# Sixteen modulation tiles of the first layer's head moved from TensorE matmuls to VectorE multiply-adds

## The reference, cut to what matters

```python
shift, scale, gate = jnp.split(jax.nn.silu(cond) @ w_mod + b_mod, 3, axis=-1)
h = rmsnorm(x, norm_g) * (1 + scale) + shift
q, k, v, z_a, xbc, z_s, dt_f, dt_b, g_a, g_s = split_cols(h @ w_in, IN_SPLITS)
```

## Time and profile before

| what | value |
|---|---|
| median of 3 runs | 2772.99 us (2772.13 to 2773.8) |
| the profiled execution | 2771.82 us, of which span 2769.8 us |
| PE busy | 2716.9 us (98% of the span) |
| DVE busy | 1965.2 us (71%) |
| ACT busy | 1481.7 us (53%) |
| HBM read and written | 226 GB/s over the span |
| granted TensorE clock, mean | 0.997 of full speed |

### The profile page before, as it was taken

How to read it: one execution, slowest core, us unless ns; L and a number is a source line. 1 busy time by engine, 2 the same in 40 slices (tenths; PEclk the granted TensorE clock), 3 DMA queues, 4 the chain that set the end, 5 groups by cost and what they waited for, 6 DMA issues and landing times.

```text
span 2769.8 us, 39481 instructions
## 1 busy us (share of the span) xinstructions
PE 2716.9 (98%) x15824; PEld 2325.3 (84%) x15824; DVE 1965.2 (71%) x2292; ACT 1481.7 (53%) x2145; POOL 172.1 (6%) x242
## 2 busy tenths in 40 slices
PE   7999999999999999999999999999999999999998
PEld 4898898888887888877779998889888888988886
DVE  2487888887997455599975788888866644555555
ACT  3366877785333455534335577687744344545443
POOL 0000101101000000000010011110110000000000
PEclk9999999999999999999999999999999999999999
DMA  9956666566887645578985566566566654555665
GB/s 394 344 179 213 226 223 206 207 221 240 316 305 258 200 141 166 191 287 293 336 303 172 203 220 221 198 225 223 191 222 242 243 199 158 174 161 178 203 220 167
DMA packets 175670, 627.89 MB, mean 227 GB/s; under 512 B 21028, under 2 KB 23332, under 8 KB 175104
## 3 DMA queue, kind: packets, MB, share of 16 engines
q1 hardware_dynamic: 154944, 557.19, 57.4%
q0 software_dynamic: 10672, 33.30, 4.1%
q10 hardware_dynamic: 9872, 34.89, 4.0%
HBM read 611.37 MB, written 13.93 MB: 226 GB/s over the span
## 4 chain that ended last, share of the span: by engine, by line
PE 84%; DVE 9%; issue 2%; DMA 2%; ACT 1%; SPq 0%; DVEq 0%; POOLq 0%; POOL 0%; ACTq 0%
PE PM L472 17%; PE PM L484 17%; PE PM L473 17%; PE PM L488 7%; PE PM L477 7%; PE PM L478 7%; PE A L764 6%; DVE arena L549 3%; DVE Zt L549 2%; DVE w_l L450 2%; DMA Zt<-in_w_mod 2%; PE PM L761 1%; DVE X L1568 1%; PE A L761 1%; ACT w_h L445 1%
## 5 line engine op out<-in xcount | busy, mean ns | idle before, releaser
L450 DVE TENSOR_TENSOR w_l<-raw,w_h 128x1024 fp32r<-128x1024 f32 (+1 forms) x880 | 1059.0, 1220 | 680.2 <-ACT w_h L445 673.3
L445 ACT ACTIVATE w_h<-raw 128x1024 fp32r<-128x1024 f32 (+1 forms) x880 | 904.9, 1046 | 802.1 <-PE PM L484 546.3
L472 PE MATMUL PM<-w_h,hT_h 128*128 128x512 f32 x1408 | 563.5, 400 | 2.1 <-issue 1.9
L473 PE MATMUL PM<-w_h,hT_l 128*128 128x512 f32 x1408 | 549.3, 390 | 0.0
L477 PE MATMUL PM<-hT_h,w_h 128*128 128x256 f32 x1920 | 479.1, 287 | 3.3 <-DVE X L1568 1.7
L478 PE MATMUL PM<-hT_l,w_h 128*128 128x256 f32 x1920 | 470.3, 283 | 0.0
L472 PE MATMUL PM<-w_h,Z 128*128 128x512 f32 x1016 | 399.3, 393 | 1.1 <-issue 0.8
L473 PE MATMUL PM<-w_h,Z 128*128 128x512 f32 x1016 | 395.7, 389 | 0.0
L484 PE MATMUL PM<-w_l,hT_h 128*128 128x512 f32 x1408 | 377.8, 390 | 3.0 <-DVE w_l L450 3.0
L477 PEld LDWEIGHTS PM<-hT_h,w_h 128*128 128x128 f32 x1920 | 367.2, 191 | 11.3 <-issue 6.9
L478 PEld LDWEIGHTS PM<-hT_l,w_h 128*128 128x128 f32 x1920 | 367.8, 192 | 2.1 <-issue 1.4
(11 more groups left out here) (204 smaller groups left out, 2230.5 us busy)
## 6 DMA issues: line engine op xcount, KB each, us to landing
raw<-in_w_in SPq DMA_DIRECT2D x608, 512.0 KB, 4.4
raw<-in_w_ps SPq DMA_DIRECT2D x128, 512.0 KB, 4.5
Zt<-in_w_mod SPq DMA_DIRECT2D x96, 512.0 KB, 13.2
arena<-in_w_mod SPq DMA_DIRECT2D x80, 512.0 KB, 6.4
Zt<-acs_scratch ACTq DMA_DIRECT2D x64, 512.0 KB, 4.8
raw<-in_w_pa SPq DMA_DIRECT2D x64, 512.0 KB, 4.1
raw<-in_w_out SPq DMA_DIRECT2D x64, 512.0 KB, 5.7
arena<-in_states POOLq DMA_DIRECT2D x16, 512.0 KB, 7.2
```

Source lines behind the costliest of these rows:

```text
L445: act.activation(w_h[:, k % RING, :, 0:n], half_raw(k, n), ACT.Copy).then_inc(hi_ready, 1)
L450: dve.tensor_tensor(w_l[:, k % RING, :, 0:n], half_raw(k, n), w_h[:, k % RING, :, 0:n].bitcast(F32), ALU.subtract).then_inc(lo_ready, 1)
L472: pe.matmul(tok_out(s), hi[:, kt, tk], wh, start=kt == 0, stop=False, skip_group_check=True)
L473: pe.matmul(tok_out(s), lo[:, kt, tk], wh, start=False, stop=False, skip_group_check=True)
```

## The change

In blocks 2 and 3 the tiles with odd kt (33, 35, ..., 47 and 49, 51, ..., 63: sixteen tiles) go through `tile_add` on DVE, into accumulators in the two halves of `X`. The even tiles stay with PE, and accumulate in `A` as before. Behind half 11 and half 19 PE runs `mod_sum` for the block, which adds DVE's accumulators onto what the even tiles left in the bank (`start` is false for it). ACT's copy of the block waits for that sum. On DVE the adds stand behind the low part of the same half as they stood behind on PE. SP's loads keep their order.

```diff
 def on_dve(m):
-    q = m // KT
-    return q == 11 or 3 < q < 10
+    q, kt = divmod(m, KT)
+    return q == 11 or 3 < q < 10 or q in (2, 3) and kt % 2 == 1
...
+SUMMED = (2, 3, 4, 5, 6, 7, 8, 9, 11)
...
         def mod_sums(q, s):
+            if q in (2, 3):
+                return X[:, 2 * MOD_N * (3 - q) + s * MOD_N:2 * MOD_N * (3 - q) + (s + 1) * MOD_N]
...
             held = tile_loaded(dve, m)
+            if first and q in (2, 3):
+                dve.wait_ge(s_("xT_copied"), 4)
...
                     mm = pe.matmul(A[32 * j:32 * j + 32, 3, 0:256], ones2[:, s, :], mod_sums(q, s)[:, j * 256:(j + 1) * 256],
-                                   start=s == 0, stop=s == 1, skip_group_check=True)
+                                   start=s == 0 and q > 3, stop=s == 1, skip_group_check=True)
...
-            if q < 4 or q == 10:
+            if q not in SUMMED:
                 act.wait_ge(mod_used, max(i for i, m in enumerate(PE_TILES) if m // KT == q) + 1)
             else:
-                act.wait_ge(s_("mod_summed"), q - 3 - (q == 11))
+                act.wait_ge(s_("mod_summed"), SUMMED.index(q) + 1)
...
                 if KT <= m < GROUP_TILES:
-                    sp.wait_ge(mod_used, m - Z_SLOTS + 1)
+                    tile_done(sp, m - Z_SLOTS)
...
                     if L == 0:
                         for m in Z_RUN.get(at, ()):
-                            mod_tile(pe, m)
+                            if not on_dve(m):
+                                mod_tile(pe, m)
+                        if at in (11, 19):
+                            mod_sum(pe, 2 + at // 16)
...
                     lo_half(dve, base + lc, 2 * g + ii, N if lc else 2 * NH)
+                    if L == 0:
+                        for m in Z_RUN.get(at, ()):
+                            if on_dve(m):
+                                tile_add(dve, m)
                     for step in st.get(at, ()):
                         step()
```

More of the change, by code:

```diff
@@ L141, in on_dve @@
 def on_dve(m):
-    q = m // KT
-    return q == 11 or 3 < q < 10
-DVE_TILES = [m for m in RAW_TILES.values() if on_dve(m)]
-PE_TILES = list(range(GROUP_TILES)) + [m for m in RAW_TILES.values() if not on_dve(m)]
+    q, kt = divmod(m, KT)
+    return q == 11 or 3 < q < 10 or q in (2, 3) and kt % 2 == 1
+DVE_TILES = [m for m in range(GROUP_TILES) if on_dve(m)] + [m for m in RAW_TILES.values() if on_dve(m)]
+SUMMED = (2, 3, 4, 5, 6, 7, 8, 9, 11)
+PE_TILES = [m for m in range(GROUP_TILES) if not on_dve(m)] + [m for m in RAW_TILES.values() if not on_dve(m)]
 PE_TILES = sorted(PE_TILES + list(range(FILLERS, FILLERS + KT)))
@@ L537, in tile_add @@
             held = tile_loaded(dve, m)
+            if first and q in (2, 3):
+                dve.wait_ge(s_("xT_copied"), 4)
             if first and q == 6:
-                dve.wait_ge(s_("mod_summed"), 1)
+                dve.wait_ge(s_("mod_summed"), SUMMED.index(4) + 1)
             if first and q == 9:
```

## The result

The changed kernel takes 2784.11 us (median of five runs, 2782.38 to 2785.0); the kernel before, on the same chip beside it, 2772.13 us (five runs, 2771.45 to 2773.8). The ratio is 1.0043 [1.0031, 1.0055], so 12.0 us slower. The forecast was 2778.2 us with a range to 2781.8: right in sign, but +5.2 us are less than half of the 12.0. The profiled execution took 2782.38 us, the fastest of the five, with a span of 2780.5 us: +10.7 us against the span of before.

What follows compares the result with a forecast made beforehand. The prediction took tile 63's landing as bounding the head, with DVE becoming the bound after the change: half 20 starts at 122.5 instead of 117.4, +5.1, plus 0.1 handover, +5.2 us, 2778.2 against the median; range 2775.2 to 2781.8.

Steps and rivals of the forecast that it cites:

- The work taken off PE: Head, blocks 2 and 3: net 6.4 us less PE work, worth 0 by itself because tile 63 lands no sooner.
- The price of an add: On DVE: 2.39 us per added tile, 1.32 for a block's first, assumed the same from `Zt` as from `arena`.
- DVE's cover: PE's idling of 5.7 us from 63.2, before tile 32, costs 0, since DVE does not need that PE work.
- The deep hollow: Load queue at half 17: late issue at 91.9 leaves it empty, so all that follows lands 1.7 us later.
- the queue stands still from 92.3 to 94.0: Half 17's load goes out at 91.9 as the queue runs empty; 2.1 us until data flows, later landings 1.7 us late.
- The term of 1.7 + 0.5 us: Load queue delay: 1.7 us at half 17 and a further 0.5 us at half 20, whose load waits for half 15.
- my chain: DVE's sequence of adds, low parts and waits from tile 33 at 63.3 to the last add's end at 121.4.
- the rule of five slots: Half 17's load may go out only when the low part of half 12 is done, moving it from 79.1 to 91.9.
- The lower one: Lower bound: no queue gap, DVE waits only for tile 63, then adds and sum; +2.9 us, perhaps +2 after later waits.
- The upper one: Upper bound: the queue gap at half 17 is 2 us longer, giving +7.2 us, or +9 with the clock.
- gap or clock worse: Rival: half 17's queue gap 1 to 2 us longer, or clock falls before the last sum; +6.8 to +9, chance 0.27.
- 0 for the last sum: PE's clock after about 2.8 us of idling before the last sum: 0 or +1.6 us, taken as 0.

Runs made afterwards that it cites:

- the last runs: Changed kernel with tiles 13 and 15 of both blocks kept on PE: 2778.92 us; with tile loads one half earlier 2773.47 us, two halves earlier 2772.99 us.
- tiles_early2: Changed kernel with the tile loads of blocks 2 and 3 two halves earlier in SP's order: 2775.49 us, 1.0012.
- late_raw: Kernel before, with SP waiting one half longer for a slot for the loads of halves 10 to 23: 2773.36 us, 1.0004.
- only_block3: Changed kernel with only block 3's eight odd tiles on DVE, block 2's staying on PE: 2780.15 us, 1.0031.
- defer2: Changed kernel with every odd tile added two halves later on DVE: 2781.98 us, 1.0035.

## Why the prediction was half right

| step | forecast | measured |
|---|---|---|
| DVE stands at tile 33 until | 63.3 | 63.15 |
| `mod_scale` of block 1 | 68.9 | 68.46 |
| end of the adds of block 2 | 90.8 | 93.5 |
| load of half 17 goes out | 91.9 | 94.77 |
| tile 51 has landed | 96.8 | 100.66 |
| end of the adds of block 3 | 121.4 | 127.3 |
| half 20 starts on PE | 122.5 | 128.5 |
| `mod_cols` of block 3 | 125.6 | 131.45 |

**Right.** The work taken off PE was worth nothing, by the last runs too. DVE became the engine that bounds the head, from its stop at tile 33 on. The price of an add, 2.40 us against 2.39, holds for reads from `Zt`. The late start of block 2's tiles on PE lay under DVE's cover: DVE waits for neither ACT nor PE between 59 and 128 us. The deep hollow came where it was forecast, at half 17, and cost 2.1 us against 1.7. Behind 131 us all is a constant shift.

**The step that failed** is "the queue stands still from 92.3 to 94.0", with all before it taken as full and 0.5 us for all behind it. The term of 1.7 + 0.5 us measured 8.1, by the landing of tile 63: 3.4 us before half 17 where I had 0, 2.1 at half 17, and 2.6 behind it where I had 0.5. Up to `mod_scale` of block 1 my chain was right, and it implied the number that shows the error: the low part of half 7 done near 72.3 (66.2 + 2.39 + 2.53 + 1.14), measured 72.1. Half 12's load waits for it, and had gone out at 64.36 before. I applied the rule of five slots at half 17 and not at halves 12 and 13. Half 13's waits for the low part of half 8 and went out at 76.10 instead of 65.91. So fewer loads came in from 70 to 84 us, DVE stood 2.6 us for tiles 43 and 45, and the load of half 17 went out 2.9 us later than I had it. The miss of 5.9 us at the end of the adds comes apart as: 2.9 us at half 17's issue; 1.0 us because tile 51 landed 5.9 us behind that issue and not 4.9; 1.7 us of waits for tiles 59 and 61 (1.49 and 0.22), that is the same loop at halves 20 to 22, which went out at 106.84 and later, where I had 0.5 us and no wait; 0.3 us of small differences over 26 us.

**The bounds.** The lower one, +2.9 us with a queue that never runs empty, is near what tiles_early2 measured (+3.2), but by luck: I had two adds and the sum behind tile 63's landing at 116.86, and there tile 63 lands at 113.78 and DVE's own work ends the head. The upper one, +7.2 and +9 with the clock, took one gap and made it 2 us longer. A gap that stops the engine which must close it isn't bounded by one gap's length. Here it came back: hollows from 70, 94 and 106 us on. The rival "gap or clock worse" had the right mechanism and was priced at one turn.

**The clock.** I took 0 for the last sum, and 0 it was in the profiled execution, which is luck, since I had one row on each side and no reason to choose. PE idled 3.19 us before 127.47 and the windows behind it stayed at 1.00, as this one of the changed kernel shows, set beside one under DVE's cover:

```profile
127.50:129.00 1.50, 1.50 (x20) 0.92 (x21) 1.50 (x2) 0.39 (x2) 0.00 (x0) 1.00 0.04 11
68.00:74.00 6.00, 5.20 (x27) 4.42 (x28) 5.93 (x15) 1.67 (x3) 0.00 (x0) 0.50 0.76 285
```

But the equal idle of 3.18 us before 93.66 was followed by 0.76 and then 0.50 at 94 to 98 us (windows above): the clock was 1.00 from 94 to 95 us and 0.54 from 95.0 to 95.5, so it fell when PE had been at work again for more than 1 us. And in the kernel before, 2.8 us had been enough at 38.75. The Trainium skill's "No PE-idle gaps >~3µs" (TensorE: Matmul & The Clock Gate, Why this matters for your kernels) fits as a caution; these stretches, on both sides of 3 us, don't sort by it.

**What stays open.** Why the change's median lies 1.7 us above its profiled execution; a fall of the clock before the last sum would be of that size (1.6 us by the forecast), but only the one execution has a trace. What the 2.2 us are that the adds cost with early tile loads and the last tiles on PE. And why, from 78 to 82 us, only 268 and 274 GB/s arrive although the DMA engines count as 0.82 and 0.98 busy. The number of loads sent out does not explain it: six loads went out between 76.1 and 79.2 us, and the first of them landed at 81.2. The issues from 75 to 79.6 us, with KB each and the median time to landing in us:

```profile
Zt<-in_w_mod SPq DMA_DIRECT2D x4, 512.0 KB, 8.0
raw<-in_w_in SPq DMA_DIRECT2D x2, 512.0 KB, 6.8
```

So late issues alone do not account for the whole of the first hollow.

## What to carry to other kernels

Where one engine frees the slots of an in-order load queue and also waits for data of that queue, its work and its waits together can cost more than their sum: neither alone cost more than 3.2 us here, both together 12. Before moving work to such an engine, write down for every load in the stretch when its slot comes free in the changed kernel, and compare it with when the queue would run low, the first time and not only the worst time. If it does, first put the loads that nobody's lateness holds up ahead of those that wait for a slot.

## What the runs showed of the hardware that was not expected

- The DMA share does not give the rate: 268 GB/s at a share of 0.82 and 274 at 0.98 (78 to 82 us of the changed kernel, with up to six loads of 512 KB issued and not landed), against 407 at 1.03 in the kernel before. From 96 to 100 us of late_raw it was 266 at 0.82. The cause is open.
- The granted clock doesn't follow the length of PE's idle stretch alone: it fell after or within stretches of 2.8 us (kernel before), 3.18 us (changed kernel, over 1 us after PE had started again), 4.57 us (only_block3) and 7.00 us (defer2), and stayed at 1.00 after 3.19 us (changed kernel).
